# Second feed-forward product of a fused decoder layer: from 32 plain panels to a seven-product block form on tile pairs and token halves

## What is computed

```python
D_MODEL = 1024; SEQ = 512; D_FF = 4 * D_MODEL
def reference(x, ..., g_mlp, w_ff1, w_ff2):
...
        x = x + merged @ w_out[l]
        h2 = rms_norm(x, g_mlp[l])
        x = x + jnp.square(jax.nn.relu(h2 @ w_ff1[l])) @ w_ff2[l]
    return x
```

## Time and profile before

| what | value |
|---|---|
| three runs | 748.69, 747.30, 747.87 us; median 747.87 |
| span of the profiled execution | 745.8 us (the runs' times hold 1.5 to 2.9 us more, what lies around the span) |
| busy share PE, PEld, DVE, ACT, POOL | 99%, 86%, 70%, 56%, 24% |
| granted TensorE clock, mean | 1.000 |
| DMA | 70.95 MB, mean 95 GB/s |
| FF1 pairs | about 418 to 568 us |
| FF2 | 568.3 to 742.6 us |

### The profile page before, as it was taken

One profiled execution on the slowest core, in us unless ns is written; L12 is line 12 of the kernel. 1 busy time (PEld: TensorE's weight loads), 2 busy tenths in 40 slices (PEclk: granted clock), 3 DMA queues, 4 the chain that ended last, 5 costly groups with the idle time before them and its releaser, 6 DMA issues.

```text
span 745.8 us, 11968 instructions
## 1 busy us (share of the span) xinstructions
PE 738.1 (99%) x4398; PEld 642.8 (86%) x4398; DVE 523.5 (70%) x999; ACT 416.9 (56%) x777; POOL 178.8 (24%) x192
## 2 busy tenths in 40 slices
PE   9999999999999999999999999999999999999998
PEld 9998977877997878777888999999998888888886
DVE  5478888779986877757768988888887444435343
ACT  7768377756778886654366565565565323232230
POOL 3110346424555544300022323222230000000000
PEclk9999999999999999999999999999999999999999
DMA  9622222101111021112532333343333232333322
GB/s 332 250 80 57 68 87 69 46 29 58 58 58 58 29 76 39 57 46 96 198 111 88 96 104 113 114 114 91 107 89 112 86 112 85 103 95 91 108 84 113
DMA packets 21833, 70.95 MB, mean 95 GB/s; under 512 B 2448, under 2 KB 3600, under 8 KB 21520
## 3 DMA queue, kind: packets, MB, share of 16 engines
q1 hardware_dynamic: 21776, 70.19, 29.8%
HBM read 68.08 MB, written 2.10 MB: 94 GB/s over the span
## 4 chain that ended last, share of the span: by engine, by line
PE 84%; DVE 7%; ACT 5%; issue 2%; DMA 1%; POOL 0%; SPq 0%; DVEq 0%; POOLq 0%
PE psum L1830 23%; PE psum L1832 23%; PE psum L1831 23%; PE psum L1838 5%; PE psum L2027 4%; PE psum L2004 2%; PE psum L2005 2%; DVE w_lo L1311 1%; DMA x2T<-in_xT 1%; ACT w_hi L929 1%; DVE x2T L1812 1%; ACT h L929 1%; ACT q_st L929 1%; DVE prob L1525 1%; DVE x2T L1678 1%
## 5 line engine op out<-in xcount | busy, mean ns | idle before, releaser
L929 ACT ACTIVATE w_hi<-stage 128x512 fp32r<-128x512 f32 (+4 forms) x149 | 118.4, 802 | 113.0 <-DMA stage<-in_panels 106.7
L1311 DVE TENSOR_TENSOR w_lo<-stage,w_hi 128x1024 fp32r<-128x1024 f32 (+4 forms) x74 | 76.4, 1037 | 110.4 <-ACT w_hi L929 106.4
L1830 PE MATMUL psum<-hT_hi,w_hi 128*128 128x256 f32 (+1 forms) x324 | 113.5, 350 | 0.8 <-DVE q_st L1467 0.6
L1831 PE MATMUL psum<-hT_lo,w_hi 128*128 128x256 f32 (+1 forms) x324 | 107.3, 331 | 0.0
L1830 PE MATMUL psum<-a_hi,w_hi 128*128 128x512 f32 x256 | 99.7, 389 | 0.2 <-issue 0.2
L1831 PE MATMUL psum<-a_lo,w_hi 128*128 128x512 f32 x256 | 99.6, 389 | 0.0
L1832 PE MATMUL psum<-a_hi,w_lo 128*128 128x512 f32 x256 | 99.6, 389 | 0.0
L1832 PE MATMUL psum<-hT_hi,w_lo 128*128 128x512 f32 (+1 forms) x264 | 90.6, 343 | 0.0
L1116 ACT ACTIVATE prob<-prob,neg_max 128x128 f32<-128x128 f32 (+3 forms) x96 | 53.8, 560 | 35.3 <-DVE neg_max L1525 34.6
L893 POOL TENSOR_TENSOR w_lo<-stage,w_hi 128x512 fp32r<-128x512 f32 x46 | 59.6, 1299 | 36.2 <-ACT w_hi L929 36.1
L1830 PE MATMUL psum<-t_hi,w_hi 128*128 128x256 f32 x240 | 67.9, 283 | 0.0
(11 more groups left out here) (276 smaller groups left out, 1708.4 us busy)
## 6 DMA issues: line engine op xcount, KB each, us to landing
stage<-in_panels SPq DMA_DIRECT2D x104, 512.0 KB, 3.6
xT_in<-in_xT SPq DMA_DIRECT2D x8, 260.0 KB, 5.0
x_in<-in_x SPq DMA_DIRECT2D x4, 512.0 KB, 7.2
phi<-in_phi SPq DMA_DIRECT2D x2, 1024.0 KB, 6.4
x2T<-in_xT SPq DMA_DIRECT2D x1, 2048.0 KB, 8.8
out_xT<-x2T SPq DMA_DIRECT2D x8, 256.0 KB, 2.0
stage<-in_panels SPq DMA_DIRECT2D x8, 212.0 KB, 5.1
stage<-in_panels SPq DMA_DIRECT2D x4, 408.0 KB, 3.1
```

Of the source, the lines that this page charges most:

```text
L929: return nc.scalar.activation(dst, src, ACT.Copy, scale=scale)
L1311: tt_op(w_lo[:, p % SLOTS, cols], stage[:, p % SLOTS, cols], hi_place(p)[:, cols].bitcast(F32), ALU.subtract)\
L1830: mm(dst, a_h, b_h, start=start, stop=False)
L1831: mm(dst, a_h, b_l, start=False, stop=False)
```

## The change

FF2 gets the block form of FF1. The 4096 inputs are taken in 8 quads of four 128-tiles and the 1024 outputs in two halves of four blocks. A step takes one quad and one half: two panels of 512 x 256 weights, cut into four blocks, seven products of 2 x 2 `product` each, so again 84 matmuls of 128x256. There are 16 steps (`STEPS`) in four passes (`PASSES`): half 0 with quads 0 and 1, half 1 with quads 0 to 4, half 0 with quads 2 to 7, half 1 with quads 5 to 7. In a pass the seven products pile up in seven banks; at its end they are added to `x2T` in combinations (`take_first`, `add_firsts`, `add_u`, `add_lasts`). Below, n counts FF1 pairs 0 to 14 and goes on with the steps, n = 15 + m, m = 0 to 15.

The weight sums, rounds and remainders of the pairs now go on for all 16 steps. The activations need sums too, per group i of two tiles (16 groups): `scale_act` moves from DVE to POOL (one instruction of 128x1024 per group) and starts inside FF1; POOL makes four sums of 256 tokens each (`sum_forms`, three instructions); ACT rounds (`round_forms`, three), DVE makes remainders (`low_forms`, three: 256, 512 and 1024 columns). Three quads' sums are kept (`FORM_SLOTS`). Tables say at which n or m a group is dealt with. The volume loaded is the same, 32 panels of 512 KB. The last pass is stored in five transfers.

```diff
+PASSES = (0, range(0, 2)), (1, range(0, 5)), (0, range(2, 8)), (1, range(5, 8))
+FORM_SLOTS = 3
+EARLY_FORMS = {0: [2], 3: [5], 4: [7], 5: [9], 9: [11], 10: [13], 11: [15]}
+LATE_FORMS = {0: [3], 1: [4], 3: [6], 4: [8], 8: [10], 9: [12], 10: [14]}
+FIRST_FORMS = {12: [0], 13: [1]}
+SCALED_AT = {5: [0, 1], 6: [2, 3], 7: [4, 5], 8: [6, 7], 9: [8], 10: [9], 11: [10], 12: [11], 13: [12], 14: [13],
+             15: [14], 16: [15]}
...
+            def scale_act(i):
...
+                nc.gpsimd.tensor_tensor(a, a, rstd_bc[:, None, :].to_broadcast([P, 2, S]), ALU.mult)\
+                    .then_inc(act_scaled, 1)
...
+            def sum_forms(i):
...
+                link(nc.gpsimd.tensor_tensor(t[:, 0::2, :], flat[:, :, half_s:],
+                                             flat[:, 0, :].rearrange("p (a t) -> p a t", a=2), ALU.subtract))
+                link(nc.gpsimd.tensor_tensor(t[:, 1, :], flat[:, 1, half_s:], t[:, 0, :], ALU.subtract))
+                nc.gpsimd.tensor_tensor(t[:, 3, :], flat[:, 1, 0:half_s], t[:, 1, :], ALU.subtract)\
...
+            def add_u(r):
...
+                nc.gpsimd.tensor_tensor(x, x, pass_u[:, :, :].rearrange("p a (d t) -> p a d t", d=2), ALU.add)\
...
+            sum_s34(0)
+            for n in range(NSTEPS):
+                m = n - PAIRS
+                for i in LATE_FORMS.get(m, []):
+                    sum_forms(i)
+                if n + 1 < NSTEPS:
+                    sum_s34(n + 1)
+                for i in SCALED_AT.get(n, []):
+                    scale_act(i)
+                for i in FIRST_FORMS.get(n + 1, []) + EARLY_FORMS.get(m + 1, []):
+                    sum_forms(i)
+                if m >= 0 and closes[m] and n + 1 < NSTEPS:
+                    add_u(STEPS[m][0])
...
+            for m, (r, _, _) in enumerate(STEPS):
+                n = PAIRS + m
+                low_last(n)
+                if m and closes[m - 1]:
+                    add_lasts(STEPS[m - 1][0])
+                for i in EARLY_FORMS.get(m, []):
+                    low_forms(i)
+                if n + 1 < NSTEPS:
+                    sum_s12(n + 1)
+                    low_first(n + 1)
+                if closes[m]:
+                    add_firsts(r)
+                for i in LATE_FORMS.get(m, []):
+                    low_forms(i)
+                if n + 1 < NSTEPS:
                     low_s(n + 1, 0)
                     low_s(n + 1, 1)
...
+            add_u_here(len(PASSES) - 1)
+            add_lasts(len(PASSES) - 1)
```

More of the change, by code:

```diff
@@ L61, in panel_list @@
     panels += [("w_ff1", 0, KT, i * P, P) for i in range(FF // P)]
-    panels += [("w_ff2", i, 1, 0, D) for i in range(FF // P)]
+    for _, half, quad in STEPS:
+        panels += [("w_ff2", 4 * quad, 4, half * 4 * P + m * 2 * P, 2 * P) for m in range(2)]
     return panels
@@ L316, in hybrid_layer @@
     assert FF1 % SLOTS == 0 and FF2 % SLOTS == 0 and PLAIN == 2 and PAIRS % 2
-    Y_ORDER = [4, 5, 6, 7, 0, 1, 2, 3]
+    NSTEPS = PAIRS + len(STEPS)
+    opens = [m == 0 or STEPS[m - 1][0] != STEPS[m][0] for m in range(len(STEPS))]
+    closes = opens[1:] + [True]
+    left_open = [sum(not closes[i] for i in range(m + 1)) for m in range(len(STEPS))]
+    final_use = {quad: m for m, (_, _, quad) in enumerate(STEPS)}
     bank = Banks()
@@ L396, in hybrid_layer @@
         released[OUT0 + i] = ("full", ("out", i))
[L397 to L403, removed]
+    for f in range(PLAIN):
+        released[FF1 + f] = ("full", ("ff1", f))
+    for n in range(NSTEPS):
+        released[FF1 + PLAIN + 2 * n] = ("product", (n, 1))
+        released[FF1 + PLAIN + 2 * n + 1] = ("product", (n, 6))
     with ExitStack() as ctx:
@@ L781, in _, with store @@
                 load_panel(p)
[L782 to L785, removed]
+            def store(d0, n, tok):
+                sp.dma_start(out[d0 * P:(d0 + n) * P, tok].rearrange("(k p) t -> p k t", p=P),
+                             x2T[:, d0:d0 + n, tok]).then_inc(stored, 16)
+            first, second = slice(0, half_s), slice(half_s, S)
+            for r in (2, 3):
+                d0 = PASSES[r][0] * 4
+                wait_drained(sp, ("y", r, 1))
+                store(d0, 2, first)
+                wait_drained(sp, ("y", r, 4))
+                store(d0 + 2, 2, second)
+                wait_drained(sp, ("y", r, 5))
+                store(d0, 2, second)
+                if r == 2:
+                    wait_drained(sp, ("y", r, 6))
+                    store(d0 + 2, 2, first)
+                else:
+                    wait_drained(sp, ("y", r, 6))
+                    store(d0 + 2, 1, first)
+                    wait_drained(sp, "y_last")
+                    store(d0 + 3, 1, first)
+            sp.wait_ge(stored, 16 * 9)
         CONSTS_ALL = 3 + 1 + 2 * H + 2 + 1
@@ L1193, in round_first @@
                 wait_loaded(se, p)
-                wait_full(se, ("pair", n - 1, 0) if n else ("out", KT - 2))
+                if n:
+                    wait_product(se, n - 1, 1)
+                else:
+                    wait_full(se, ("out", KT - 2))
                 copy(w_hi[:, 2, :], stage[:, p % SLOTS, :]).then_inc(form_hi, 1)
@@ L1219, in square_u @@
                 nc.scalar.activation(act[:, f, :], act[:, f, :], ACT.Square).then_inc(squared, 1)
[L1221 to L1224, removed]
[L1225 removed]
             def round_s12(n):
[L1228 removed]
+                if n:
+                    wait_product(se, n - 1, 4)
+                else:
+                    wait_full(se, ("out", KT - 1))
                 se.wait_ge(s12_done, 2 * n + 2)
@@ L2190, in _ @@
                 full(block_product(dst[:, second], block[6], a22_lo, *t[3]), ("pair", n, 3))
[L2192 to L2204 removed]
+            block_at = [4, 5, 7, 0, 6, 1, 2]
```

327 lines of the change are left out of this document (234 added, 93 removed).

## The result

| | before | changed |
|---|---|---|
| median (lowest to highest) | 747.59 us (746.93 to 748.69) | 831.62 us (830.50 to 832.43) |
| ratio, 95% interval | | 1.1122 [1.1106, 1.1137] |
| span of the profiled execution | 745.8 | 828.8 |
| granted TensorE clock, mean | 1.000 | 0.961 |

A forecast was written before the change was run, and what follows sets the result against it. PE, busy 99%, was taken as the bound, waiting wherever DVE and POOL's shared demand exceeds 10.085 us per round. 34.4 + 49.5 - 12.8 = +71.1 us; 745.8 + 2.1 + 71.1 = 819.0, range 775 to 845.

The forecast's parts named there:

- PE's gain of 12.8 us: FF2's matmuls as 16 steps at FF1's pair rate: 161.4 us instead of 174.2, if PE never waits.
- Turns of DVE and POOL: SBUF-SBUF DVE instructions never overlap POOL's; per 512 columns a turn costs 0.55 us of DVE or 1.15 of POOL.
- FF1, 34.4 us: PE's waits in FF1 rounds n = 5 to 14, where DVE and POOL demand exceeds 10.085 us: 34.4 us in sum.
- The 1.7 of n = 14: FF1's last round, with a demand of 11.75 us against 10.085: 1.7 us of excess.
- FF2, 49.5 us: PE's waits in FF2 steps m = 0 to 13, where DVE and POOL demand exceeds 10.085 us: 49.5 us in sum.
- the rounds with two forms: FF2 m = 3, 4, 9, 10, each with two activation groups' sums and remainders: 15.71 us, +5.6 each, 22.5 together.
- those with one: FF2 m = 5, 8, 11, each with one activation group's sums and remainders: 11.48 us, +1.4 each, 4.2 together.
- the rounds of the pass ends: FF2 m = 6 and 7, 12 and 13, one pass end per pair: 22.75 us for 20.2, +2.6 each pair, 5.2 together.
- rival 1: Over FF1 and FF2, surplus demand carries over to slack rounds, so only total demand counts: 782 us (775 to 798); chance 0.20.
- rival 2: In FF2's DVE list, POOL's new work does not shut out DVE's, so the kernel gets faster: 739 us; chance 0.08.
- rival 3: PE's clock drops to 1.2 GHz from idling; six steps lose some 6 us each beyond their wait: 855 us; chance 0.07.
- What would show it: Signs: FF1 ends some 34 us later, FF2 takes 205 to 215, PE waits for L1865 and L1926, L1865 3 us, L1017 over 2.4.

The follow-up runs named there:

- second mixed kernel: Kernel before, but FF2's last 16 panels in seven-product form, with scalings, activation sums, pass-end additions and the steps' weight sums on DVE: 742.47 us, ratio 0.9930.

## Why the prediction was right, and where it was off

- **PE's gain of 12.8 us** (16 x 10.085 against 174.2): right as a rate. In the second mixed kernel, where nothing holds PE up, its last steps end 10.08 us apart, six times in a row. By the Trainium skill (TensorE: Matmul & The Clock Gate, "Back-to-back issue gap") the estimate was 19.1; the measured rate decides.
- **Turns of DVE and POOL**: right, and shown by taking POOL's reads away (799.2), the work away (797.0), and by putting the work alone into the old kernel (774.3; its pairs 6 to 9 take 13.9 to 14.2 us, as in the changed kernel). The Trainium skill (SBUF — State Buffer, "Who interferes with whom") has the two shut each other out for the whole instruction; the trace agrees, 3.40 us for an L1865 of 1.22 when it is queued behind a scaling.
- **FF1, 34.4 us**: right. Rounds n = 5 to 13 were put at 32.7 and measured 33.0; n = 5 to 8 take 13.78, 14.15, 14.03 and 14.01 for the 14.05. The 1.7 of n = 14 fall into PE's first step of FF2.
- **FF2, 49.5 us**: too low. With n = 14 it is 51.2 forecast and 62.3 measured; this is why 831.6 came out and not 819.0. The mechanism held here too: the rounds with two forms come out at 24.4 for 22.5, those with one at 3.2 for 4.2. The term that was too small is the price of a handover, 2 x 0.55 for L1856 and L1858 and 1.15 for L1009. Those prices are of engines that both have a queue. In FF2 nothing lies between these three, and each waits for the one before:

```profile
649.85 0.69 DVE L1856 TENSOR_TENSOR s_sum<-stage 128x512 f32<-128x512 f32 x1
650.57 0.69 DVE L1858 TENSOR_TENSOR s_sum<-s_sum,stage 128x512 f32<-128x512 f32 x1
651.34 1.29 POOL L1009 TENSOR_TENSOR s_sum<-stage,s_sum 128x512 f32<-128x512 f32 x1 [6.74 <-DVE s_sum L1858]
652.66 2.31 DVE L1865 TENSOR_TENSOR w_lo<-stage,w_hi 128x1024 fp32r<-128x1024 f32 x1 [1.40 <-POOL s_sum L1009]
```

  From 649.85 to 652.66 are 2.81 us where 2.25 were priced, 0.56 per round. The same stretch takes 2.78 to 2.82 us in twelve of the 14 rounds m = 0 to 13 and 3.80 in m = 6 and 12, so an estimate from these rows is 14 x 0.56 = 7.8 of the 11.1 us. By kind of round it fits those with two forms (2.2 for 1.9 missed) and not those with one (1.7, where 1.0 less than forecast was measured), and no run took the handover away by itself. In FF1 the gap is as long, but the additions out of PSUM, priced by themselves at 2.2, stand in it, which is why its rounds came out. The rest lies at the start of FF2 and in the rounds of the pass ends (11.1 for 5.2). Of the latter the trace shows two things: behind m = 7's L1009 POOL goes straight into sums listed under m = 8 (at 721.13), so these lengthen round m = 7 and not m = 8, and PE's step m = 14 loses 1.6 us to the low clock. What remains was not traced.
- **The surplus is not carried over** (rival 1, 0.20): right, 831.6 lies far from 782, and each kind of heavy round shows its own excess in the table.
- **No turns, faster** (rival 2, 0.08): refuted by all of the above. Even the kernel with writes in place of POOL's new work is at 753.7, not 739: PE waits 14 us in it, where 4 were put (its weight sums still take turns).
- **PE's clock falls as well** (rival 3, 0.07): it fell, to 0.961 in the mean, where the forecast had it full and each matmul at 0.120; that part of the forecast was wrong. But the rival's price of 6 us a step was wrong too: with the clock held up in FF1 and at the two longest waits, the time moved by 2.1 us at most.
- **What would show it**: FF1 ended 33.6 us later, and L1865 took 3.4 us behind a scaling (2.3 on average); the wait for L1865 came as named. L1017 took 3.4 only as the second of two scalings (four times), and 2.34 to 2.42 else. FF2 took 223.7 us, outside the 205 to 215 named. L1926 was not the one PE waited for: it was L1924 of the same group, once, and L1871.

## What to carry to other kernels

Before giving elementwise work to an idle engine, read in the trace whether the engine that is nearly late runs two-input SBUF instructions: then the time of the moved work is added to that engine's, and on POOL it is longer (the 16 scalings cost 34.6 us there and 21.0 on DVE). Sum a round's demand by who waits for whom, not by busy shares: 81% and 43% were a full pair here. A form that saves PE time is worth only as much as its operands come free, and in a stage where DVE has time it can be had for part of the work alone.
